# A three-layer transformer kernel: output projections in steps of 4 k-tiles by 512 columns, token tiles finished one by one, memory heads in pairs, a packed first weight slot

## What is computed

```python
# block 1: one wide input projection, three mixers, gated sum, output projection
h = rmsnorm(x, g_pre)
gq,gk,gv,ga,gz,dq,dk,dv,iq,ik,iw,dz,xq,xz,gates = split_cols(h @ w_in)
merged = s_gla*(y_gla @ w_gla_out) + s_dsa*(y_dsa @ w_dsa_out) + s_mem*(y_mem @ w_x_out)
x = x + rmsnorm(merged @ w_o, g_post)
# block 2: two layers (mLSTM, then sliding-window attention), each with memory heads and a feed-forward
for l in range(2):
    h = rmsnorm(x, g_mix_pre[l])
    mk, mv = split(rmsnorm(mem, g_mem[l]) @ w_mem_kv[l])
    main, mq = mixer_l(h)
    s = einsum('bqhd,bmhd->bhqm', mq, mk) * 64 ** -0.5        # 4 memory heads of 64, 256 memory tokens
    mo = einsum('bhqm,bmhd->bqhd', softmax(s), mv)
    x = x + rmsnorm(concat([main, mo]) @ w_out[l], g_mix_post[l])
    gate, up = split(rmsnorm(x, g_ffn_pre[l]) @ w_ffn_in[l])
    x = x + rmsnorm((silu(gate) * up) @ w_ffn_out[l], g_ffn_post[l])   # 2816 rows
    if l == 0: k_sh, v_sh = shared_kv(x, g_kv, w_kv)
```

## Time and profile before

| | us |
|---|---|
| median of 3 runs | 2212.89 (2209.84 to 2217.92) |
| the profiled execution, its own time | 2215.03 |
| its span, first to last instruction | 2213.2 |
| PE busy | 2091.2 (94%) |
| DVE busy | 902.9 (41%) |
| ACT busy | 804.2 (36%) |
| DMA | 23.8% of 16 engines on the queue of the slots |

### The profile page before, as it was taken

One profiled execution on the slowest core, in us unless ns is written; L12 is line 12 of the kernel. 1 busy time (PEld: TensorE's weight loads), 2 busy tenths in 40 slices (PEclk: granted clock), 3 DMA queues, 4 the chain that ended last, 5 costly groups with the idle time before them and its releaser, 6 DMA issues.

```text
span 2213.2 us, 28389 instructions
## 1 busy us (share of the span) xinstructions
PE 2091.2 (94%) x12192; PEld 1806.3 (82%) x12192; DVE 902.9 (41%) x1056; ACT 804.2 (36%) x1181; POOL 11.3 (1%) x21
## 2 busy tenths in 40 slices
PE   7999999899999999899988999999898798999998
PEld 5798888678898687889867888899897586888897
DVE  3366265554342233423445333322556524333322
ACT  4443232443243332434544333322436634333221
POOL 0000000000000000000000000000000000000000
PEclk9999999999999999999989999999898899999999
DMA  5522122122242122222212223223231012232322
GB/s 170 131 77 69 46 93 91 65 77 96 95 153 91 43 96 95 93 96 77 77 39 72 105 85 109 87 103 108 74 115 57 1 58 70 92 103 88 113 96 77
DMA packets 29030, 192.52 MB, mean 87 GB/s; under 512 B 3673, under 2 KB 3801, under 8 KB 7554
## 3 DMA queue, kind: packets, MB, share of 16 engines
q1 hardware_dynamic: 25810, 180.15, 23.8%
q0 software_dynamic: 3120, 10.88, 1.8%
HBM read 187.35 MB, written 3.67 MB: 86 GB/s over the span
## 4 chain that ended last, share of the span: by engine, by line
PE 89%; DVE 6%; ACT 3%; issue 1%; DMA 1%; SPq 0%; DVEq 0%; ACTq 0%
PE PS L418 27%; PE PS L420 26%; PE PS L419 26%; PE PS L517 1%; DVE X L1403 1%; PE PS L885 1%; PE PS L532 1%; PE PS L525 1%; DVE wlo L1339 1%; PE PS L536 1%; PE PS L900 1%; DMA raw<-in_stream 1%; PE PS L652 0%; ACT slg L1314 0%; PE PS L822 0%
## 5 line engine op out<-in xcount | busy, mean ns | idle before, releaser
L418 PE MATMUL PS<-hhi,whi 128*128 128x512 f32 x1424 | 561.5, 394 | 10.5 <-DVE hlo L1369 8.8
L420 PE MATMUL PS<-hhi,wlo 128*128 128x512 f32 x1424 | 559.7, 393 | 0.0
L419 PE MATMUL PS<-hlo,whi 128*128 128x512 f32 x1424 | 558.9, 392 | 0.0
L1339 DVE TENSOR_TENSOR wlo<-raw,whi 128x2048 fp32r<-128x2048 f32 x123 | 281.9, 2292 | 547.7 <-ACT whi L917 547.4
L917 ACT ACTIVATE whi<-raw 128x2048 fp32r<-128x2048 f32 x167 | 319.1, 1911 | 220.2 <-PE PS L420 219.4
L418 PEld LDWEIGHTS PS<-hhi,whi 128*128 128x128 f32 x1424 | 268.6, 189 | 73.1 <-issue 9.5
L420 PEld LDWEIGHTS PS<-hhi,wlo 128*128 128x128 f32 x1424 | 268.5, 189 | 59.1
L419 PEld LDWEIGHTS PS<-hlo,whi 128*128 128x128 f32 x1424 | 268.5, 189 | 58.9
L418 PE MATMUL PS<-whi,ahi 128*128 128x256 f32 x704 | 194.3, 276 | 0.0
L419 PE MATMUL PS<-wlo,ahi 128*128 128x256 f32 x704 | 194.3, 276 | 0.0
L420 PE MATMUL PS<-whi,alo 128*128 128x256 f32 x704 | 194.3, 276 | 0.0
(11 more groups left out here) (338 smaller groups left out, 3116.0 us busy)
## 6 DMA issues: line engine op xcount, KB each, us to landing
raw<-in_stream SPq DMA_DIRECT2D x167, 1024.0 KB, 4.9
gpost<-in_gposts POOLq DMA_DIRECT2D x5, 512.0 KB, 4.2
X<-in_x SPq DMA_DIRECT2D x4, 512.0 KB, 8.8
X<-in_x POOLq DMA_DIRECT2D x1, 2048.0 KB, 8.7
out<-X SPq DMA_DIRECT2D x4, 512.0 KB, 2.8
bias_line<-linet POOLq DMA_DIRECT2D x1, 1536.0 KB, 35.1
tbias<-bias_line POOLq DMA_DIRECT2D x1, 1024.0 KB, 6.8
memx<-in_mem POOLq DMA_DIRECT2D x1, 1024.0 KB, 10.4
```

The lines of the kernel that those rows point to most:

```text
L418: nc.tensor.matmul(out, lh, rh, start=(k == 0), stop=False)
L419: nc.tensor.matmul(out, lh, rl, start=False, stop=False)
L420: return nc.tensor.matmul(out, ll, rh, start=False, stop=(k == n_k - 1))
L1339: V_.tensor_tensor(wlo[:, s % 2], raw[:, s % 2], whi[:, s % 2], ALU.subtract).then_inc(lo_ready[s % 2], 1)
```

## The change

- `slots()` and `wide_pairs()`: the slots of `w_o`, `w_out_*` and `w_ffn_out_*` are used in pairs that cover the same rows and two neighbouring blocks of 256 columns. SP's first transfer of a pair takes the first 4 k-tiles of both, the second the last 4. SP's loop is written out.
- `wide_out` (one per engine) takes the place of `gemm_tokens` with `mixed`/`take_output`/`residual`, and of the loop over `w_ffn_out`. A step is up to 4 k-tiles by 512 columns in one PSUM bank per token tile; half 0 (columns 0 to 511) uses banks 0 to 3, half 1 banks 4 to 7. The two steps over the 6-row group have 4 and 2 k-tiles. All four token tiles run in each step; in the last step each finished tile signals `tile_psum`, and squares, root, residual and norm are done tile by tile.
- The wait for the split activations moves into the matmuls (`arrival(k)`): `w_o` no longer needs k-tiles 4 to 7 for its first step, and the projection of layer 0 no longer waits for all of `y_lo`.
- `memory_pairs`: logits of two heads interleaved (rows 0 to 63, rows 64 to 127, banks of their own), four buffers `xp2`, transposes into the head's own banks, `values` of two heads interleaved (output partitions 0 to 63 and 64 to 127 of one bank), one copy for both. In layer 1 DVE's three splits of `so` stand behind the last `scale`.
- The first slot holds ik once: a GEMM of one group; `ikT`'s upper half is copied by a DMA on POOL's queue (`ik_doubled`).

```diff
-    out.append([("w_in", 0, KT, O_IK, 64, 0), ("w_in", 0, KT, O_IK, 64, 64),
-                ("w_in", 0, KT, O_GA, 16, 128), ("w_in", 0, KT, O_IW, 8, 144)])
+    out.append([("w_in", 0, KT, O_IK, 64, 0), ("w_in", 0, KT, O_GA, 16, 64), ("w_in", 0, KT, O_IW, 8, 80)])
...
-        for c in range(4):
-            for r in range(0, FFT, KT):
-                full(f"w_ffn_out_{layer}", C * c, r0=r, rt=min(KT, FFT - r))
+        for half in range(2):
+            for r0, rt in FFN_ROWS:
+                for c in range(2):
+                    full(f"w_ffn_out_{layer}", 2 * C * half + C * c, r0=r0, rt=rt)
...
+FFN_ROWS = ((0, FFT - 2 * KT), (FFT - 2 * KT, KT), (FFT - KT, KT))
+MIX_STEPS = ((0, 1, 2, 3), (4, 5, 6, 7))
+FFN_STEPS = tuple(tuple(range(r0 + k, r0 + min(k + KT // 2, rt))) for r0, rt in FFN_ROWS for k in (0, KT // 2))
...
@@ tensor engine @@
            def wide_out(hi, lo, steps, arrival=None):
+                nonlocal n, m
+                a = 2 * (m % 2)
+                pe.wait_ge(pair_free[m % 2], m // 2)
+                for half in range(2):
+                    done = 0
+                    for j, ks in enumerate(steps):
+                        pe.wait_ge(lo_ready[n % 2], n // 2 + 1)
+                        p = n % 2
+                        w_hi, w_lo = (b_[:, p].rearrange("q (s k) c -> q s k c", s=2) for b_ in (whi, wlo))
+                        for i, t in enumerate((0, 1, 2, 3) if half else (a, a + 1, 2 - a, 3 - a)):
+                            if half == 0 and j == 0 and i == 2:
+                                pe.wait_ge(pair_free[(m + 1) % 2], (m + 1) // 2)
+                            ts = slice(t * P, t * P + P)
+                            for kk, k in enumerate(ks):
+                                if arrival and half == 0 and i == 0:
+                                    arrival(k)
+                                last = three(PS[:, 4 * half + t, :].rearrange("q (s c) -> q s c", s=2), done + kk,
+                                             sum(map(len, steps)), (hi[:, k, ts], lo[:, k, ts]), (w_hi[:, :, kk, :], w_lo[:, :, kk, :]))
+                            if half and j == len(steps) - 1 and t < NT - 1:
+                                last.then_inc(S["tile_psum"], 1)
+                        last.then_inc(slot_used[p], 1)
+                        n, done = n + 1, done + len(ks)
+                m = m + 2
+                w.next(S["wide_free"], NT)
...
@@ scalar engine, wide_out, its end @@
+                for t in range(NT):
+                    if t < NT - 1:
+                        w.next(S["tile_psum"])
+                    else:
+                        computed()
+                    squares(1, t).then_inc(S["o_sq"], 1)
+                    w.next(S["o_sq"])
+                    nc.scalar.activation(root[:, t:t + 1], part[:, t, 1:2], ACT.Sqrt, bias=first_mean[:, t:t + 1], scale=1.0 / D)\
+                        .then_inc(S["o_root"], 1)
+                    if more and t:
+                        new_root(spare, t - 1)
+                if more:
+                    new_root(spare, NT - 1)
...
@@ vector engine, wide_out, its end @@
+                for t in range(NT):
+                    take(1, t).then_inc(S["wide_free"], 1)
+                    w.next(S["o_root"])
+                    w.link(V_.reciprocal(rstd[:, t:t + 1], root[:, t:t + 1]))
+                    w.next(S["wide_free"])
+                    V_.scalar_tensor_tensor(X[:, t], o[:, t], rstd[:, t:t + 1], X[:, t], ALU.mult, ALU.add).then_inc(S["x_new"], 1)
+                    if more and t:
+                        norm_rows(t - 1, X, normed, 4, S["norm_root"], S["xn_ready"])
+                if more:
+                    norm_rows(NT - 1, X, normed, 4, S["norm_root"], S["xn_ready"])
...
@@ tensor engine @@
+            def memory_pairs(q_, slot=None):
+                def logits(u):
+                    b = 0 if u else 4
+                    for t in range(NT):
+                        for i in range(2):
+                            r = slice(MEM_HD * i, MEM_HD * i + MEM_HD)
+                            last = nc.tensor.matmul(PS[:, b + 2 * i + t // 2, (t % 2) * C:(t % 2) * C + M],
+                                                    q_[r, u, t * P:t * P + P], mk2[r, u, :], start=True, stop=True)
...
-            with sp.Fori(1, NS // 2) as i:
-                for p in range(2):
-                    sp.wait_ge(lo_ready[p], i)
-                    sp.dma_start(raw[:, p], stream[bass.ds(i, 1), p]).then_inc(raw_ready[p], 16)
+            for n in range(2, NS):
+                dst, first = raw[:, n % 2], n if n in WIDE else n - 1
+                sp.wait_ge(lo_ready[n % 2], n // 2)
+                if first in WIDE:
+                    rows = slot_rows[first:first + 2, :, (n - first) * half:(n - first + 1) * half]
+                    sp.dma_start(dst.rearrange("p (s k) c -> p s (k c)", s=2), rows.rearrange("s p c -> p s c"))\
+                        .then_inc(raw_ready[n % 2], 16)
```

More of the change, by code:

```diff
@@ L732, in _, with pair_split @@
             merge()
-            def pair_split(i):
-                if i % 2 == 0:
+            def pair_split(k):
+                if k % 2 == 0:
                     w.next(S["y_lo"])
-            for c in range(4):
-                gemm_tokens(dhi, dlo, arrival=None if c else pair_split)
+            wide_out(dhi, dlo, MIX_STEPS, pair_split)
             def feed_forward():
@@ L904, in _ @@
             attention(SW_H, logits, turn, values, memory_slots)
-            memory_attention(MEM_H, memory_parts(mqb), mv2, False)
-            for c in range(4):
-                gemm_tokens(yhi, ylo, arrival=None if c else pair_split)
+            memory_pairs(mqb)
+            wide_out(yhi, ylo, MIX_STEPS, pair_split)
             feed_forward()
@@ L980, in root_table @@
                 nc.scalar.activation(root[:, 12:13], epsv, ACT.Sqrt)
-            def o_squares(c, banks, junk):
-                if c:
-                    w.next(S["o_sq"], 2)
-                for half in (1, 0):
-                    if half == 0:
-                        w.next(S["o_half"])
-                    for t in (2 * half, 2 * half + 1):
-                        last = nc.scalar.activation(junk[:, t, :], banks[:, t, :], ACT.Square, accum_out=part[:, t, c:c + 1])
-                    last.then_inc(S["o_sq"], 1)
@@ L1387, in mixed, with wide_out, take @@
-            def mixed(loads):
+            def wide_out(o, normed, steps, loads, more=True):
                 nonlocal n, m
+                def take(half, t):
+                    cs_ = slice(half * T, half * T + T)
+                    w.next(S["o_sq"])
+                    return V_.tensor_tensor(o[:, t, cs_], PS[:, 4 * half + t, :], gpost[:, cs_], ALU.mult)
                 dve.wait_ge(S["gpost_loaded"], 16 * loads)
-                for c in range(4):
-                    take_output(o_mix, c, pair().rearrange("p b (u c) -> p (b u) c", u=2), pair_free[m % 2])
-                    if c < 3:
-                        passed()
-                n, m = n + 1, m + 1
+                for step in range(2 * len(steps) - 1):
+                    split(n + 2)
+                    n = n + 1
+                    if step == len(steps) - 1:
+                        for t in range(NT):
+                            last = take(0, t)
+                            if t % 2:
+                                last.then_inc(pair_free[t // 2], 1)
+                        V_.tensor_scalar(first_mean, part[:, :, 0], 1.0 / D, EPS, ALU.mult, ALU.add).then_inc(S["o_sum"], 1)
+                n, m = n + 1, m + 2
@@ L1737, in _ @@
             passed()
-            memory_attention(MEM_H, xp2, slot=1)
+            memory_pairs(slot=1)
             for k in range(6):
```

344 lines of the change are left out of this document (185 added, 159 removed).

## The result

The changed kernel takes 2160.85 us (median of 4 runs, 2156.48 to 2168.24), the kernel before beside it 2211.36 us (4 runs, 2206.86 to 2217.92). The ratio is 0.976, with a 95% interval of 0.974 to 0.979: faster by 2.4%. The forecast was 2162.0, in a range of 2147 to 2186.

A forecast was written before the change was run, and what follows sets the result against it. TensorE, busy 94% of the span, was taken to bound the kernel, so time goes by fewer or cheaper matmuls or less idle. The terms sum to -50.6 us: 2212.89 - 50.6 = 2162 us, range 2147 to 2186.

The forecast's parts named there:

- Matmul width: Output projections and feed-forward outputs: 1632 wide matmuls in place of 3264 narrow ones cost +3.4 us, bounds 0 to +7.
- sign of being right: Among the signs for the forecast: PE's records in the wide steps stand 228 ns apart.
- sign of being wrong: Among the signs against the forecast: starts of wide matmuls more than 235 ns apart.
- The four gaps and the end: Transitions after projections and feed-forward 0 shrink from 15.1 to 9.3 us, -22.8 for four; program end -4.4.
- The rival in which the tails shrink less: Transitions: each tile late by 2 us, so each saves 2 in place of 5.7; 2177 us, chance 0.10.
- Memory heads, layer 1: Layer 1's memory heads: 35.6 us becomes 24 to 27 with heads in pairs; -8, the slower end.
- Memory heads, layer 0: Layer 0's memory heads: same chain behind a 2.29 us weight split on DVE; -3 us.
- Starts: Idle and half clock at the start of `w_o` go, -6.5 us; layer 0's output projection waits less, -3.
- First slot: First slot: one group of 24 matmuls falls away, -5.5 us, on the path if slot 1 is ready.
- Short steps: Rival at the 2 k-tile steps: the slot after is 2 us late, four times; 2170 us, chance 0.03.
- A cheaper wide matmul: Rival for output projections: wide matmuls stream at 213.3 ns, -21 us against +3.4; 2138 us, chance 0.04.
- restart between blocks: Rival in wide matmuls: array pauses between the operand's two blocks; slower than before from 259 ns, chance 0.04.

The follow-up runs named there:

- second profile of the change: The changed kernel run again unaltered as base of the first batch; 2164.55 us, ratio to before 0.977; its profile has a span of 2157.5 us.
- the kernel that waits at the front: The change with TensorE's waits for all split activations of `w_o` and `w_out_0` back at the front of the first step; one run, 2179.72 us.

## Why the prediction was right

The sum was -50.6 and the medians differ by -50.5. The mechanisms held for nearly all terms, but the close hit of the total is luck: the width cost 7.4 us more than I charged, while the gaps gave 3.8 more, layer 1's heads 3.9 and the end 0.7, and these cancel. A gain of 1.7 at the start of `w_out_0` and the scatter of single runs lie beside them.

*Matmul width* is the term of the sum that was mis-sized. I charged 228.3 - 226.2 ns on 1632 matmuls, +3.4 us. The wide output matmuls come 233.3 ns apart, against 226.7 for two narrow ones: 1632 x 6.6 ns = +10.8, above my upper bound of 7. It shows in the two feed-forward outputs, +3.5 each. My sign of being right, 228 ns between starts, failed; the sign of being wrong, over 235, did not come either. The bound failed because I took the input loop's row for the pace of a wide matmul; that loop has two paces, and one profile showed me one. That there are two at all stood in the same trace for narrow matmuls: 113.3 ns in both feed-forward outputs, but 117.8 in a product of the shared keys (192 matmuls from 1611.61 to 1634.48 us, 22.86 us, against 22.02 in the second profile of the change). Neither the two blocks nor the change of bank is the cause. What is stays open, and so does whether the output steps are slow for the same reason as a slow loop; the output steps stream weights past stationary activations and the loops do the reverse, which I did not try to exchange.

*The four gaps and the end*: forecast 9.3 us each (10.9 at the shared keys, which had been 16.6), measured 8.05 to 8.3 after the mixers, 9.6 at the shared keys, and 5.9 for 6.5 at the end. My chain was right but for one link: I had DVE finish tile 1's norm 1.7 us after the last matmul; it finishes at 0.95. The four gaps gave 27.4 in place of 22.8. The 0.8 for a better clock in the shared keys did not come: their product still starts at 0.50, for over 3 us from 1553.6. The rival in which the tails shrink less fell with that: DVE never falls behind the 2.8 us a tile.

*Memory heads, layer 1*: -11.9 for -8. My chain gave 24 to 27 us and it is 23.7; I had taken the slow end, for last values at half clock, and by then the clock is full again. One reading in that sum was wrong: the 1.90 us of the earlier trace rows are one head's values, so two heads without overlap would take 3.8, not 1.9, and 1.9 with it, not 1.0. The overlap is what made 1.94 possible, so it is worth about 1.9 us in this term at full clock (an estimate from these two rows), and not 1.

*Memory heads, layer 0*: -3.3 for -3, right by luck. The old heads do as well there in the one profile that has them, at a full clock.

*Starts*: `w_o` -5.4 with its width term inside, that is -6.7 without; `w_out_0` -3.1; both as forecast, with the mechanism shown by the kernel that waits at the front. The half clock at the start of `w_out_0`, worth 1.7, I had not seen. *First slot*: 4.0 to 6.2 us less up to the first index score, for 5.5; that the stretch up to `w_o` gave -5.3 is luck, as the other two profiles show.

*Rivals.* Short steps don't stall (no idle of PE in either feed-forward output). A cheaper wide matmul is refuted: two narrow ones, 226.7 ns, cost less than one wide, 233.3. The Trainium skill (TensorEngine Tiling (Array Packing), Instruction Overhead) gives each matmul about 60 cycles of overhead; for these matmuls back to back the traces don't agree. No restart between blocks shows, since one run of 512 columns has the same pace.

## What to carry to other kernels

Where a norm follows a projection, finish the token tiles one by one under the last step's matmuls: of the 50 us here, by the stretches, 32 came from that, 12 from working two heads at a time where a chain through three engines set the time, 15 to 17 from shorter waits, fuller clock and one group less at the starts, and 3 from layer 0's heads, less the 11 of the dearer matmuls. Check that nothing in the queues of the finishing engines waits for the end of the step, since one such wait took back 40 of the 50 us. Choose the matmul's width by measured spacing, and measure it in the loop where it will run: here 2 x 256 columns beat 512 by 3% in the feed-forward outputs, while in the short mixer outputs the shorter gap behind 512 columns made up for it.
